# Encoder layer with a mixture of experts: expert rows loaded during the overflow blocks, overflow rows patched in by gathers, five last-stage tiles summed on TensorE

## What is computed

```python
h = h + parallel_mixer(rmsnorm(h, g_mix), ...)            # gated mixing and neighbourhood attention
h = h + memory_cross_attention(rmsnorm(h, g_xattn), ...)
h = h + hierarchical_moe(rmsnorm(h, g_moe), ...)          # top-1 group of 4, top-2 of its 8 experts
return rmsnorm(h, g_final)
```

## Time and profile before

| | |
|---|---|
| median of 3 runs | 1269.18 us (1268.66 to 1271.07) |
| the profiled execution's own time | 1269.01 us |
| its span, first to last instruction | 1267.5 us |
| TensorE busy | 1151.4 us, 91% of the span |
| VectorE, ScalarE, GpSimd busy | 672.0, 468.2, 266.6 us |
| mean granted TensorE clock | 0.964 of full speed |
| chain that ended last | PE 82%, DVE 5%, DMA 3%, ACT 3% |

### The profile page before, as it was taken

One profiled execution on the slowest core, in us unless ns is written; L12 is line 12 of the kernel. 1 busy time (PEld: TensorE's weight loads), 2 busy tenths in 40 slices (PEclk: granted clock), 3 DMA queues, 4 the chain that ended last, 5 costly groups with the idle time before them and its releaser, 6 DMA issues.

```text
span 1267.5 us, 18202 instructions
## 1 busy us (share of the span) xinstructions
PE 1151.4 (91%) x6250; PEld 956.9 (75%) x6250; DVE 672.0 (53%) x1279; ACT 468.2 (37%) x972; POOL 266.6 (21%) x373
## 2 busy tenths in 40 slices
PE   6999999999989999999999999999986999999800
PEld 5888888878878888888889788778775788887600
DVE  6333233311116888433366664664477988883267
ACT  6222222211005666112234333544324666763222
POOL 2322322200002222001101000000022334554244
PEclk9999999999999999999999999999996999999955
DMA  9573442863148212452222001112797999989496
GB/s 307 138 249 99 143 158 80 294 122 74 33 95 208 73 25 74 144 177 74 80 69 87 1 1 67 46 56 100 277 345 254 372 370 346 376 287 356 188 357 241
DMA packets 111206, 216.78 MB, mean 171 GB/s; under 512 B 38934, under 2 KB 51230, under 8 KB 111134
## 3 DMA queue, kind: packets, MB, share of 16 engines
q1 hardware_dynamic: 88750, 160.25, 38.3%
q0 software_dynamic: 16992, 43.02, 10.1%
q10 hardware_dynamic: 5392, 12.59, 3.0%
HBM read 169.36 MB, written 61.39 MB: 182 GB/s over the span
## 4 chain that ended last, share of the span: by engine, by line
PE 82%; DVE 5%; DMA 3%; ACT 3%; SPq 2%; issue 2%; POOL 2%; POOLq 0%; ACTq 0%; DVEq 0%
PE bank L533 17%; PE bank L535 17%; PE bank L534 17%; PE bank L2192 5%; PE bank L1991 4%; PE bank L1971 3%; PE bank L2120 3%; PE bank L2158 3%; PE bank L2178 2%; PE bank L1980 2%; PE bank L1917 2%; PE bank L2129 2%; PE bank L2054 2%; DVE at L1823 1%; DMA at<-v_att 1%
## 5 line engine op out<-in xcount | busy, mean ns | idle before, releaser
L533 PE MATMUL bank<-at,at 128*128 128x512 f32 (+1 forms) x1192 | 442.1, 371 | 5.7 <-DVE at L528 3.2
L535 PE MATMUL bank<-at,at 128*128 128x512 f32 (+1 forms) x1192 | 431.6, 362 | 0.0
L534 PE MATMUL bank<-at,at 128*128 128x512 f32 (+1 forms) x1192 | 430.9, 361 | 0.0
L533 PEld LDWEIGHTS bank<-at,at 128*128 128x128 f32 x1192 | 226.0, 190 | 40.4 <-DVE at L528 3.9
L535 PEld LDWEIGHTS bank<-at,at 128*128 128x128 f32 x1192 | 225.6, 189 | 35.1
L534 PEld LDWEIGHTS bank<-at,at 128*128 128x128 f32 x1192 | 226.1, 190 | 32.2
L528 DVE TENSOR_TENSOR at<-at,at 128x1024 fp32r<-128x1024 f32 (+2 forms) x162 | 183.8, 1148 | 87.8 <-ACT at L523 84.9
L523 ACT ACTIVATE at<-at 128x1024 fp32r<-128x1024 f32 (+2 forms) x162 | 154.4, 988 | 151.3 <-DVE at L1465 48.8
L856 POOL TENSOR_TENSOR at<-at 128x1 f32<-128x1 f32 x88 | 29.0, 330 | 530.1 <-ACT at L1200 283.4
L2192 PE MATMUL bank<-at,at 128*128 128x512 f32 x156 | 74.2, 597 | 3.3 <-ACT at L1274 3.3
L1110 ACT ACTIVATE at<-at,at 128x256 f32<-128x256 f32 (+1 forms) x96 | 51.6, 538 | 49.0 <-DVE at L1418 48.8
(11 more groups left out here) (198 smaller groups left out, 1372.9 us busy)
## 6 DMA issues: line engine op xcount, KB each, us to landing
at<-in_w_exp_gate SPq DMA_DIRECT2D x39, 512.0 KB, 7.2
at<-in_w_exp_up SPq DMA_DIRECT2D x39, 512.0 KB, 10.6
at<-in_w_exp_down SPq DMA_DIRECT2D x39, 512.0 KB, 11.3
at<-y_tok SPq DMA_DIRECT2D x24, 512.0 KB, 9.9
at<-in_w_in SPq DMA_DIRECT2D x6, 1024.0 KB, 11.4
xT_hi_all<-at POOLq DMA_DIRECT2D x12, 512.0 KB, 3.9
xT_lo_all<-at POOLq DMA_DIRECT2D x12, 512.0 KB, 5.7
at<-xT_hi_all SPq DMA_DIRECT2D x3, 2048.0 KB, 11.0
```

What stands on the lines that cost most here:

```text
L533: nc.tensor.matmul(out, w_hi, x_hi, start=(k == 0), stop=False)
L534: nc.tensor.matmul(out, w_lo, x_hi, start=False, stop=False)
L535: last = nc.tensor.matmul(out, w_hi, x_lo, start=False, stop=(k == len(terms) - 1))
```

## The change

- The expert rows of tiles 0 to 7 (`EARLY` = 8) are loaded while the overflow blocks run: once the scatters of the 32 regular blocks have landed, between the weight loads of the overflow blocks. Tiles 8 to 11 are loaded after the last scatter, as before.
- What the overflow blocks write for tokens of tiles 0 to 7 goes to an area of its own at the front of `y_tok` (`N_EARLY` = 2048 rows); GpSimd brings it over the loaded rows by two indirect DMAs a tile (`patch`), in tiles 1 to 7. Rows without overflow have an index out of bounds and are skipped. VectorE makes these indices in blocks 12 and 14.
- `y_tok` rows that an early load would read unwritten are first filled by eight copies of 2 MiB from the input `x` in HBM, on SyncE's queue ahead of `keep_rows`.
- Overflow weights have three slots, `OVER_SLOTS = (2, 6, 8)`, since the others now hold early rows. The load for overflow block n waits for block n-3 to be done. H comes back earlier, three tiles each after `y_done` 24, 25, 26 and 28.
- GpSimd waits for each overflow scatter to land, and for those of blocks 30 and 31 before the first.
- The last stage runs in the order (0, 8, 1, 9, 2, 10, 3, 11, 4, 5, 6, 7). In tiles 1, 2, 3, 4 and 6 (`BY_PE`) TensorE makes the sum in two PSUM banks: the identity times H, and two diagonal matrices with the gates (`diag`, made by VectorE in blocks 15 to 17 and after block 31) times the expert rows. ScalarE then squares each half from PSUM, GpSimd adds the two sums in a third tiny instruction, and VectorE scales each half from PSUM.

```diff
-OVER_SLOTS = (2, 6, 8, 9, 0, 1)
+OVER_SLOTS = (2, 6, 8)
+EARLY = 8
+N_EARLY = 2 * EARLY * P
+FINAL_ORDER = (0, 8, 1, 9, 2, 10, 3, 11, 4, 5, 6, 7)
+BY_PE = (1, 2, 3, 4, 6)
...
+        def y_landed(eng, t):
+            eng.wait_ge(yg_here[t % AHEAD], yg_count(t))
+            if 0 < t < EARLY:
+                eng.wait_ge(patch_here[t % 4], patch_count(t))
...
+            for k in range(2):
+                for n, rows in enumerate((a["x_prompt"][0][0:TPC * P], a["x_sample"][0][0:TPC * P])):
+                    for first in (N_EARLY + k * T, k * EARLY * P):
+                        row = first + n * TPC * P
+                        sp.dma_start(y_tok[row:row + TPC * P], rows).then_inc(y_filled, 16)
...
+            used = sp.value_load(over_n[0:1, 0:1], min_val=0, max_val=NOVER)
+            load_overflow(used, 0, 0, 23)
+            for n in range(3):
+                return_rows(n, 24 + n)
+            load_overflow(used, 1, 0, 27)
+            return_rows(3, 28)
             sp.dma_start(gf_row, a["g_final"].partition_broadcast(P)).then_inc(consts_here, 16)
+            load_overflow(used, 2, 0, 29)
+            for j in range(2):
+                sp.wait_ge(y_sent[j], 16 * NE // 2)
+            for t in (0, 1, 2):
+                load_y(t)
+            load_overflow(used, 3, 0, NE + 1)
+            for t in (3, 4):
+                load_y(t)
+            load_overflow(used, 4, 0, NE + 2)
+            for t in (5, 6):
+                load_y(t)
+            load_overflow(used, 5, 0, NE + 3)
+            load_y(7)
+            with sp.Fori(1, NOVER // RING) as i:
+                for n in range(RING):
+                    load_overflow(used, n, i, NE + RING * i + n - 2)
...
+            for j in range(2):
+                pool.wait_ge(y_sent[j], 16 * NE // 2)
             used = pool.value_load(over_n[0:1, 0:1], min_val=0, max_val=NOVER)
             for b in range(NE, NBLK):
                 with pool.If(used > b - NE):
...
                     scatter(b)
+                    pool.wait_ge(y_sent[b % 2], 16 * (b // 2 + 1))
...
+            def patch(t):
+                pool.wait_ge(yg_here[t % AHEAD], yg_count(t))
+                if t > 4:
+                    pool.wait_ge(patch_here[t % 4], patch_count(t - 4))
+                for k in range(2):
+                    pool.indirect_dma_start(out=y_g[t][k], out_offset=None, in_=y_tok,
+                                            in_offset=bass.IndirectOffsetOnAxis(ap=patch_row[:, k, t:t + 1], axis=0),
+                                            bounds_check=N_EARLY - 1, oob_is_err=False).then_inc(patch_here[t % 4], 16)
...
+            for t in (1, 2, 3):
+                patch(t)
+            for n, t in enumerate(FINAL_ORDER):
+                final_rsqrt(t)
+                if 4 + n < EARLY:
+                    patch(4 + n)
...
+            add_experts(0)
+            scale_rows(0)
+            add_experts(BY_DVE[1])
+            for t in FINAL_ORDER[1:]:
+                if t in BY_DVE[1:-1]:
+                    add_experts(BY_DVE[BY_DVE.index(t) + 1])
+                scale_rows(t)
...
+            for m, t in enumerate(BY_PE):
+                if m >= 3:
+                    pe.wait_ge(f_out, with_halves(BY_PE[m - 3]))
+                banks = SUM_BANKS[m % 3]
+                if m > 0:
+                    y_landed(pe, t)
+                for half in range(2):
+                    nc.tensor.matmul(bank[banks[half]][:], ident, H[:, t, half * HALF:(half + 1) * HALF], start=True, stop=False)
+                if m == 0:
+                    y_landed(pe, t)
+                pe.wait_ge(f_add, 2 * (m + 1))
+                for k in range(2):
+                    for half in range(2):
+                        last = nc.tensor.matmul(bank[banks[half]][:], diag[m][k], y_g[t][k][:, half * HALF:(half + 1) * HALF],
+                                                start=False, stop=(k == 1))
+                last.then_inc(sum_done, 1)
```

More of the change, by code:

```diff
@@ new lines, in return_rows, with load_y @@
+            def return_rows(n, free):
+                sp.wait_ge(y_done, free)
+                for t in range(3 * n, 3 * n + 3):
+                    sp.dma_start(H[:, t], h_kept[t * P:(t + 1) * P]).then_inc(h_moved, 16)
+            def load_y(t):
+                if t >= AHEAD:
+                    sp.wait_ge(yg_here[t % AHEAD], yg_count(t - AHEAD))
+                for k in range(2):
+                    row = N_EARLY + k * T + t * P
+                    sp.dma_start(y_g[t][k], y_tok[row:row + P]).then_inc(yg_here[t % AHEAD], 16)
@@ L1725, in overflow_index, with patch_rows @@
                 step(nc.vector.tensor_scalar(index_f, index_f, float(-P), None, ALU.add))
+            def patch_rows():
+                for k, first in ((0, 2 * T), (1, T + EARLY * P)):
+                    row = over_small[0][:, k, 0:EARLY]
+                    step(nc.vector.scalar_tensor_tensor(row, is_over[:, k, 0:EARLY], float(-FAR), token[:, k, 0:EARLY], ALU.mult, ALU.add))
+                    step(nc.vector.tensor_scalar(patch_row[:, k], row, float(first + FAR), None, ALU.add))
             def overflow_slots(n):
```

130 lines of the change are left out of this document (85 added, 45 removed).

## The result

The changed kernel takes **1282.89 us** (median of 4 runs, 1280.85 to 1283.08), the kernel before 1269.2 us (1268.66 to 1271.07) beside it: ratio **1.0102, 95% interval 1.0084 to 1.0119**. It is slower, as forecast, but by 13.7 us instead of 4.6, and lies 0.9 us outside the range of 1264 to 1282. The profiled execution took 1280.85 us, 11.8 more than that of before.

A forecast was written before the change was run, and what follows sets the result against it. It saw VectorE's 46 us end and 8.7 us row wait as winnable; late weights +8.3, restart +7.1, waits +4.1, VectorE's work -15.0 moved its end +4.6 from base 1269.0 to 1273.6, about 1274 us, range 1264 to 1282.

The forecast's parts named there:

- Late weights: Overflow blocks: early rows queued among the weights make block 37, and so the last block, 8.3 us late.
- upper bound: Overflow blocks' lateness: at most 12 us, if TensorE also falls to half clock in waits and repeats 3.6 us slowly.
- The forecast's signs: Overflow blocks and end: several-us weight waits in the last four blocks, last copy near 1211, scatters about 9 us apart.
- Scatters side by side: GpSimd in overflow blocks: waited-for scatters take 9.1 us a block against 6.98, some 6 us late alone, hidden beside late weights.
- The bound below: Overflow blocks' lateness: 0 if all 14.7 MB is hidden, needing above 600 GB/s (12.1 MB in 19.4 us).
- Walk, gathers, root: Last copy to VectorE's first scaling: 15.8 us instead of 8.7, with walk 3, six gathers 8.5, root 1.1.
- VectorE's end: Last stage: 31.2 us of VectorE work plus 7.5 of waits, ending at 1265.6 instead of 1260.95.
- TensorE's sums: Last stage: first tile's products at half clock (7 us), the rest at full, about 5.3 a tile; never late beyond counted waits.
- The rival of a lasting half clock: Last stage: TensorE stays at half clock, 10.5 us a tile, VectorE ends about 1280, time 1288; chance 0.06.
- The hidden loads (faster): Overflow blocks: weights land in time, lateness 0 and skipping 1, time 1263; chance 0.19.
- Gathers that wait for VectorE: Last stage: eight later gathers take 1.98 us each, +7.6 on GpSimd, time 1277 to 1281; chance 0.08.
- The late fill: Before the expert stage: fill not done when the experts' loads start, time 1280 and above; chance 0.03.

The follow-up runs named there:

- H last: Changed kernel with H's rows and `g_final` behind the weights of all overflow blocks instead of ahead of the third's: 1281.8 us, ratio 1.0094.
- one at a time: Changed kernel with all overflow weights ahead of early rows, 1280.2 us; without each scatter wait, 1279.2; with H behind all overflow weights, 1281.8.
- in pairs: Changed kernel without each scatter wait, plus all overflow weights ahead of early rows, 1274.7 us; or plus H behind all overflow weights, 1275.7.
- the short walk: Changed kernel with walks over 12 overflow blocks instead of 24, leaving out blocks 13 to 24: 1281.2 us, ratio 1.0095.
- the last stage alone: Kernel before with TensorE's sums in tiles 1, 3, 5, 7, 9, natural order; no early rows, fill or gathers, six weight slots: 1264.1 us, ratio 0.9954.
- rows held: Changed kernel, early rows behind the weights of blocks 35, 36 and 37 issued only when those weights have landed: 1291.4 us, ratio 1.0165.
- root first: Changed kernel, GpSimd making tile 0's root before the gathers and roots 1, 9 and 2, 10 ahead of later ones: 1282.2 us, ratio 1.0105.
- the fill alone: Kernel before plus eight HBM-to-HBM copies of 2 MiB into a tensor that nobody reads: 1269.4 us, ratio 0.9996.

## Why the prediction was wrong in size

**Late weights: the failed step.** The mechanism was right, the term was mis-sized: "8.3 us late" measured 15.3. The forecast let the backlog on SyncE's queue end at 1166.6, took block 34 as on time, and counted only what stands ahead of block 35 and what follows. The trace has, against that:
- The backlog ended later. Block 34's own weights stand behind H and `g_final` and landed at 1151.07 + 19.2 = 1170.3, 3.7 us after the queue was to be free.
- A mean rate is no landing time. From 1170.3 the three tiles and block 35's weights would have been through at 1181.9 at the forecast's 406 GB/s; they landed at 1167.85 + 15.7 = 1183.6. The DMA share was 0.78 and 0.54 in 1155 to 1165 while block 34's weights were still out. That the last bytes lay on a few of the 16 engines fits this, but no view used here shows the engines one by one.
- Behind that the rate was right. Block 35 starts 5.8 us after the forecast's landing (1183.8 against 1178.0), block 37 6.9 us after it (1203.0 against 1196.1).

Block 37's down weights landed at 1185.79 + 16.9 = 1202.7 and released its products at 1203.03; block 38 follows without a wait, so this landing sets the last copy. SyncE could not issue these weights sooner: its four issues of rows at 1177.12 took 6.33 us. The slow products of blocks 34 and 35 (1.8 and 2.7 us over 3.62), which the forecast had in its upper bound, are not on this path: block 35 then waits 4.25 us for weights that were all issued before block 34 began, and block 37 waits 1.93 us. The forecast's signs came in part: waits of several us stand at blocks 34 and 35, 1.93 us at block 37, none at 36 and 38.

What stands in front of the weights is shown by the runs. Without early rows among them the lateness is 6.8 us, with H out of the way 5.5, with both there 15.5; the two don't add, so neither 15.5 - 6.8 = 8.7 nor 15.5 - 5.5 = 10.0 is the share of one of them, and that 8.7 is near the forecast's 8.3 is luck. No run has both out of the way. Moving H behind the third block's weights does not help (16.7); moving it behind all of them does, and before the change it went there.

**Scatters side by side.** The forecast gave the scatter chain 6 us alone and counted it as hidden. Hidden it was, but its size was off too: bare, with H last, it ends 14.4 us late. The period was right (9.3 against 9.1 us), but the forecast does not say how it came to 6: six periods of 9.1 instead of 6.98 are 12.7 us. Some 7 us of each period are a landing beside a full queue. This size did not reach the sum. It bears on what a repair is worth: 2.7, 3.7 and 1.0 us one at a time, 8.2 and 7.2 in pairs. The bound below has a slip too: from 1164.0 and 2.4 us to 1187.8 are 21.4 us, not 19.4, so 12.1 MB would need 565 GB/s and not over 600; that is still far above 406.

**Walk, gathers, root.** Right: 15.9 us from last copy to first scaling against 15.8. The walk behind the landing (1218.95 + 2.6 = 1221.55) took GpSimd 3.9 us with hand-over, where the forecast took 3, and the short walk shortened it by 2.1 for twelve `If`s, 0.18 us each. VectorE's walk stands as 4.98 us of idle time, and was hidden behind GpSimd's six gathers. By the Trainium skill, "Advanced Engine Details and Errata", Control Flow Timing, the walk would take an estimated 1.8 us; the trace is above that on both engines, and the trace decides.

**VectorE's end.** Right: 38.5 us against 38.7. The waits were 3.39 and 3.38 where 2.6 was forecast, 0.46 and 0.73 where 0.75 was, and none at the end.

**TensorE's sums.** Right in the main: the first took 5.29 us and the next three 3.60 at full clock. The last took 4.62, behind a wait of 1.87 us for VectorE and with the clock at a mean of 0.67 and 0.91 in 1256 to 1264. TensorE never set the end, since all of VectorE's waits are for GpSimd. The rival of a lasting half clock is refuted.

**The rivals.** The hidden loads (faster) failed on the weights, as weighed. Gathers that wait for VectorE were there in part: of the eight later gathers four took 1.95 to 2.05 us. In the page's row of the source line:

```profile
L1056 POOL DMA_INDIRECT at<-y_tok,at x14: 992/1002/2053, 1225.5 to 1252.6; - x14
```

The four began while a VectorE instruction with two inputs in SBUF was running (three scalings, one addition), and each ended 0.9 us after that instruction. The Trainium skill, "SBUF — State Buffer", A bandwidth-pool intuition that's wrong, says such a DMA waits for the end of VectorE's instruction: these four agree. The six ahead of VectorE's restart took 1.0 to 1.1, as did two with VectorE idle, one beside a scaling from PSUM (1.05) and one that started in the same moment as an addition (1236.48). The four cost GpSimd 4 us, a part of which sits in the waits of 3.4. The late fill is refuted by its run.

## What to carry over

When a transfer is moved into a stretch that looks free, list every DMA that stands ahead of each block's weights with the block's due time, down to the first one, and not only behind the point where the new bytes come in; the landing of the last piece, 15.7 to 19.2 us here, is the number to set against the lead, not the mean rate. Before repairing one late chain, look for another that ends at the same time: of the edits here, single ones gave up to 4 us, not clear of noise, and pairs 7 to 8. And try the parts of a change apart: the last stage alone was faster by 5 us, which the whole hid.

## What the runs showed of the hardware

- In a full queue the down weights of blocks 34 to 37 landed 15.7 to 19.2 us after their issue, and SyncE's issues were slow too: nine of 512 KB took 19.45 us.
- Behind waits of 3.2 to 11.4 us for weights the 16 products of a block took 5.29 to 6.60 us instead of 3.62, at a mean granted clock of 0.70 and 0.59 in the two windows shown. Behind waits under 2 us they took 3.72 at most. Waits of 2.0 to 2.8 us were followed by either: 5.40 behind 2.01 and 2.17 us ("rows held", "root first"), 3.72 behind 2.01, 2.36, 2.38 and 2.82 us.
- A scatter of one block lands after 2.4 to 2.6 us on an idle queue and after 6.5 to 7.9 us beside a full one.
- A gather takes 1.0 us; one that begins while VectorE runs an instruction with two inputs in SBUF ends 0.9 us after that instruction, and takes 1.94 to 2.05 us when it begins just behind its start.
- A walk over 17 unused `If`s shows as 4.98 us of idle time on VectorE and 5.37 on TensorE; written out on GpSimd, twelve `If`s fewer saved 2.1 us.
- Copies of 16.8 MB from HBM to HBM beside TensorE's products kept the DMA engines at a mean share of 0.95 to 1.00 from 800 to 850 us ("the fill alone") and cost no time.
